# Outputs of three tiles of the last pair of heads in an idle projection bank, and gates ahead of the low parts of y

## What is computed

```python
# layer A: windowed attention, blocks of 128 queries, keys: window + context
s_lat = einsum('bqkgd,bjkd->bkgqj', qb, kb) * scale      # masked to |i-j| <= 128
s_ctx = einsum('bqkgd,bckd->bkgqc', qb, kc) * scale
p = softmax(concatenate([s_lat, s_ctx, s_sink]))
o = p_lat @ vb + p_ctx @ vc
y = (o * silu(g)) @ w_out
# layer B: neighbourhood attention, 8 rows x 16 columns of keys, with a relative bias
s = einsum('bnqhd,brnjhd->bhnqrj', q_r, k_reg) * scale + bias
p = softmax(concatenate([s, s_ctx]))
y = ((p_lat @ v_reg + p_ctx @ vc) * silu(g)) @ w_out
```

## Time and profile before

| | |
|---|---|
| median of 3 runs | 2119.71 us (2117.7 to 2121.08) |
| profiled execution | 2125.02 us, its span 2123.2 us |
| granted TensorE clock, mean | 0.979 |
| PE busy | 95% of the span |
| DVE, ACT, POOL busy | 52%, 38%, 38% |

### The profile page before, as it was taken

How to read it: one execution, slowest core, us unless ns; L and a number is a source line. 1 busy time by engine, 2 the same in 40 slices (tenths; PEclk the granted TensorE clock), 3 DMA queues, 4 the chain that set the end, 5 groups by cost and what they waited for, 6 DMA issues and landing times.

```text
span 2123.2 us, 36592 instructions
## 1 busy us (share of the span) xinstructions
PE 2011.9 (95%) x14756; PEld 1668.3 (79%) x14756; DVE 1096.0 (52%) x2212; ACT 814.4 (38%) x1584; POOL 811.5 (38%) x586
## 2 busy tenths in 40 slices
PE   7999999999998899999999899799999999999895
PEld 6878878877877788888888788678888888887674
DVE  5457467658556565556666624533344344344625
ACT  4100100100125365556666502534544545545501
POOL 3333333333346523212222145544444344354456
PEclk9999999999999999999999899899999999999997
DMA  4322332322222300101001233121111111112142
GB/s 163 136 82 90 109 98 72 119 90 70 79 90 97 103 34 21 33 34 34 34 34 57 85 108 115 65 75 50 45 46 50 48 43 50 50 41 78 53 145 113
DMA packets 48325, 155.99 MB, mean 73 GB/s; under 512 B 5280, under 2 KB 8224, under 8 KB 48032
## 3 DMA queue, kind: packets, MB, share of 16 engines
q1 hardware_dynamic: 47152, 152.40, 21.7%
q10 hardware_dynamic: 1008, 1.27, 0.2%
HBM read 132.94 MB, written 20.71 MB: 72 GB/s over the span
## 4 chain that ended last, share of the span: by engine, by line
PE 85%; DVE 7%; issue 3%; POOL 3%; ACT 2%; DMA 1%; POOLq 0%; DVEq 0%; SPq 0%; ACTq 0%
PE psum L821 23%; PE psum L822 21%; PE psum L823 21%; PE psum L996 8%; PE psum L957 7%; PE psum L973 5%; DVE win L1317 1%; PE psum L830 1%; POOL out_tile L798 1%; PE psum L923 1%; POOL w_lo L660 1%; POOL rstd L683 1%; DVE logits L1529 0%; DVE u_lo L1563 0%; DVE x_hat L1431 0%
## 5 line engine op out<-in xcount | busy, mean ns | idle before, releaser
L821 PE MATMUL psum<-u_hi,w_hi 128*128 128x512 f32 (+1 forms) x1440 | 547.5, 380 | 13.3 <-DVE u_lo L1440 7.5
L658 POOL CAST w_hi<-w_raw 128x1024 fp32r<-128x1024 f32 x140 | 155.8, 1113 | 982.2 <-DMA w_raw<-weights_in 982.2
L822 PE MATMUL psum<-u_lo,w_hi 128*128 128x512 f32 (+1 forms) x1440 | 528.2, 367 | 0.0
L823 PE MATMUL psum<-u_hi,w_lo 128*128 128x512 f32 (+1 forms) x1440 | 527.6, 366 | 0.0
L660 POOL TENSOR_TENSOR w_lo<-w_raw,w_hi 128x1024 fp32r<-128x1024 f32 x140 | 348.9, 2492 | 11.2
L821 PEld LDWEIGHTS psum<-u_hi,w_hi 128*128 128x128 f32 x1440 | 274.8, 191 | 66.8 <-issue 8.9
L823 PEld LDWEIGHTS psum<-u_hi,w_lo 128*128 128x128 f32 x1440 | 274.7, 191 | 45.4
L822 PEld LDWEIGHTS psum<-u_lo,w_hi 128*128 128x128 f32 x1440 | 275.3, 191 | 39.2
L1192 ACT ACTIVATE logits<-logits,neg_max 128x640 f32<-128x640 f32 (+2 forms) x288 | 226.1, 785 | 66.0 <-DVE neg_max L1529 64.9
L1210 ACT ACTIVATE prob_t<-psum 128x320 f32<-128x320 f32 (+1 forms) x288 | 119.0, 413 | 330.2 <-PE psum L973 330.1
L1201 ACT ACTIVATE logits<-logits,row_rec 128x640 f32<-128x640 f32 (+1 forms) x288 | 217.7, 770 | 0.0
(11 more groups left out here) (142 smaller groups left out, 3006.0 us busy)
## 6 DMA issues: line engine op xcount, KB each, us to landing
w_raw<-weights_in SPq DMA_DIRECT2D x140, 512.0 KB, 3.6
w_ada<-w_ada_in SPq DMA_DIRECT2D x48, 512.0 KB, 3.5
residual<-act_buf SPq DMA_DIRECT2D x4, 2048.0 KB, 7.4
tab<-bias_tab_in SPq DMA_DIRECT2D x16, 496.5 KB
res<-residual SPq DMA_DIRECT2D x26, 256.0 KB, 3.5
act_buf<-x_t_in SPq DMA_DIRECT2D x8, 512.0 KB, 13.5
out<-out_tile SPq DMA_DIRECT2D x8, 512.0 KB, 2.6
staged<-a_y SPq DMA_DIRECT2D x6, 640.0 KB, 2.9
```

The costliest lines, as they stand in the source:

```text
L658: pool.tensor_copy(w_hi[:, slot, :], w_raw[:, slot, :]).then_inc(w_hi_done, 1)
L821: pe.matmul(out, wh, xh, start=first, stop=False)
L822: pe.matmul(out, wh, xl, start=False, stop=False)
L823: return pe.matmul(out, wl, xh, start=False, stop=last)
```

## The change

The outputs of tiles -1, 0 and 1 go to the first 128 columns of a `pj` bank, which no projection uses in those rounds, and no longer wait for logits. The output of tile -1 waits instead for the last projection that used the bank to have been read; and PE waits in round 3, ahead of the first projection chunks, until the output of tile 1 has been gated. In all rounds of the last pair DVE does `gate_output` ahead of `low_y`.

```diff
+    def out_bank(layer, g):
+
+        aside = 0 <= g - (TILE0[layer] + (PAIRS - 1) * TILES[layer] - 1) < 3
+        return (pj[EARLY[layer][1].index % 2][:, 0:P], True) if aside else (ps_out, False)
...
@@ outputs
-            pe.wait_ge(logit_done, min(s + 6, STEP0[layer] + 2 * PAIRS * TILES[layer]))
+            out, aside = out_bank(layer, g)
+            if not aside:
+                pe.wait_ge(logit_done, min(s + 6, STEP0[layer] + 2 * PAIRS * TILES[layer]))
+            elif t == TILES[layer] - 1:
+                after(pe, pj_free[EARLY[layer][1].index % 2], EARLY[layer][1].index // 2)
...
-                    mm = pe.matmul(ps_out[r, :], v[:, tile, r], prob_t[:, g % 2, h, c, :], start=c == 0,
+                    mm = pe.matmul(out[r, :], v[:, tile, r], prob_t[:, g % 2, h, c, :], start=c == 0,
...
@@ attention (TensorE)
                 if pair == PAIRS - 1:
+                    if t == 3:
+                        pe.wait_ge(gated, g - 1)
...
@@ gate_output
-            out, y = ps_out, y_tile(layer, y_buf[layer][pair % 2], t)
+            (out, _), y = out_bank(layer, g), y_tile(layer, y_buf[layer][pair % 2], t)
...
@@ attention (VectorE)
-                if pair == PAIRS - 1:
-                    for k in {1: (0,), 2: (1, 2), 3: (3, 4), 4: (5, 6)}.get(t, ()):
-                        low_y(layer, k)
                 if layer == 0:
                     rope_due(pair, t)
                 for c in ended(PARTS[layer][pair][t]):
                     take(layer, c)
                 if g > first:
                     gate_output(layer, g - 1)
+                if pair == PAIRS - 1:
+                    for k in {1: (0,), 2: (1, 2), 3: (3, 4), 4: (5, 6)}.get(t, ()):
+                        low_y(layer, k)
```

## The result

The changed kernel took 2129.92 us (median of 6 runs, 2125.95 to 2131.83), the kernel before 2118.72 us (6 runs, 2117.7 to 2121.19). The ratio is 1.0048, 95% interval 1.0036 to 1.006. Timed again on another occasion it was 1.0044 (1.003 to 1.0057). So it is 10 to 11 us slower (11.2 by these medians, 10.2 by the ratio). The prediction said slower by 4.7 us, less than half of that, and its range ended at 2129.0 us, 0.9 us under the measured median.

The account below looks back on a forecast made before the run. A ring of engines in which only PE's waits cost time was taken as the bound. -2.5 + 3.4 us in B, -2.2 + 2.5 in A and +3.5 for the clock gave +4.7 on 2119.7: 2124.4 us, range 2118.5 to 2129.0.

Parts of the forecast that it names:

- the loss of these two rounds without the clock: Rounds 3 and 4: low parts behind the gate delay the next transposes, 3.4 us in B and 2.5 us in A.
- The whole sum at an unchanged clock: Both layers' gains until round 3 and losses behind it: +1.2 us, bounds -0.8 to +3.5.
- the clock term: Three new PE gaps of 2 us and more, each bringing 1.2 GHz in two of three cases: +3.5 us.
- The gain until round 3: Rounds 0 to 2: outputs in PE's gaps and earlier gates bring round 3's transposes forward, 2.5 us in B, 2.2 in A.
- The first: Rival: new stalls are there but the clock stays up or shorter early idle pays for it; 2120.9 us; chance 0.20.
- The second: Rival: outputs in the old gaps keep the upper clock through rounds 0 to 3 and behind new gaps; 2116.4 us; chance 0.12.
- The third: Rival: all three gaps bring the lower clock, and low parts meet a second such stretch per layer; +8.7 us, 2128.4; chance 0.10.
- The fourth: Rival: outputs wait anyway for something else, so nothing is seen there; +3 or so; chance 0.58 together with the forecast.

Follow-up runs that it names:

- the clock held up: Changed kernel plus 6 matmuls by a tile of zeros in TensorE's new gaps of rounds 4 and 5: 2124.18 us, ratio 1.0026 to the kernel before.
- the gap filled: Changed kernel, low parts before gate in rounds 3 and 4, unread matmuls before round 3's transposes: 0.9977, again 0.9985; with outputs in their old place 0.9996.
- the bank alone: Changed kernel with low parts ahead of the gate as before, outputs of tiles -1, 0 and 1 still in the projection bank: 2117.74 us, ratio 0.9992.

## Why the prediction was right or wrong

**The waits were forecast rightly, place by place.** TensorE no longer stood idle ahead of the outputs in rounds 0 to 2, the gate behind TensorE's work kept the low parts waiting in rounds 3 and 4, and the copy behind them held up the next transposes. The prediction put the loss of these two rounds without the clock at 3.4 + 2.5 = 5.9 us. Stretch II with the clock held up is 60.9, against 55.6 as the mean of the two traces of before: 5.3 us. The whole sum at an unchanged clock, +1.2 us, has no run of its own. The nearest, with the clock held up behind these gaps but not in round 3, was 5.5 us slower than before.

**The step that failed is the clock term, "3 gaps x 2/3 x 1.75 = 3.5 us".** Stretch II of the changed kernel is 66.3 us in the mean of two traces, with the clock held up 60.9: 5.4 us. Seven of eight gaps brought the lower level, and there were four gaps, not three: the fall behind round 5 of A, which the earlier trace rows show in the kernel before, was not there in its second trace, so that it was no property of before that one could leave out of the sum. The price of one, 1.5 us between two rows above, was near the 1.75 taken. The term also had nothing for round 3, whose work took 1.8 us longer in the mean of two traces (12.6 against 10.8).

**The gain until round 3 was a little too large.** The prediction gave it as 4.7 us at the transposes of round 3, 2.5 in B and 2.2 in A. There it is 3.7 us (44.8 before, 41.1 changed, each the mean of two traces). At the outputs of round 3, behind the round's work, 1.9 us of it are left (stretch I, 55.6 and 53.7).

**What took the rest is in part open.** In ten traces nothing fills the gap of round 3, and 19 of their 20 pieces of work of round 3 lie below 1.00 (0.54 to 0.82), in the kernel before as in the others, behind one long gap (4.45 us), a short one (1.84 us) or gaps in other places. In nine of these traces this work takes 11.7 to 13.5 us in both layers together; with the gap filled it is 8.6 us in each of three. So the lower level costs about 3 us there, and filling wins them back, but that the change made this worse by lengthening the gap is not shown: the changed kernel's two traces took 11.7 and 13.5 us, those of before 12.0 and 9.7, and the last, the only one with 1.00 in B, makes most of the 1.8 us. That low parts done sooner meet GpSimd's casts (5.01 us instead of the 2.87 of the first trace) put the transposes of A off by about 1 us, but the run without that gained nothing in time.

Put together: -3.7 + 1.8 + 5.3 + 5.4 = +8.8 us, and timed were 10.4 and 11.2. The four traced executions themselves are only 7.7 us apart in the mean (2121.4 and 2129.1 us), since the first of before was a long one. So the stretches hold all of the difference of these executions, and what is missing against the medians is which executions were traced.

**The rivals.** The first (the clock stays up) fell in every trace of the changed kernel. The second asked for 1.00 through rounds 1 to 5; the changed kernel's own windows show 0.65 and 0.73 in round 3 and less than 1.00 in three of four behind it. Its estimate of round 3's work at the upper level, 3.9 and 4.9 us, was right: with the gap filled it took 3.82 and 4.77. Its 0.50 for both rounds 0 and 1 of A was read too far, since the window of the earlier trace rows ends with round 0; the stretch behind it, 1169.5 to 1174.2, has 0.59 with TensorE busy for 4.63 of 4.70 us. The third was nearest in size (+8.7), by the same mechanism as the forecast with all gaps falling. The fourth (nothing to be had from the wait for logits) falls with the traces: the outputs begin behind the transposes without the 1.9 us of idle, and TensorE reaches the transposes of round 3 sooner with the bank alone. In the times the bank's worth could not be told from nothing (0.9992, with 1.0001 as the upper end). The page of the Trainium skill "TensorE: Matmul & The Clock Gate", section "HAM oscillation — how this bites in real kernels", warns of longer gaps only. Here gaps of 1.78 to 2.33 us were followed by clocks of 0.60 to 0.70 in seven of eight cases, and the measurement decides. The gap of 4.46 us ahead of round 3, which the prediction did not foresee, is of the kind that the section warns of, and 0.65 was granted behind it.

## What to carry to other kernels

On an engine with a fixed order, put work that needs nobody ahead of an instruction that waits for a slow producer, and behind one whose producer is long done; here the same swap costs 9 to 11 us through the rounds with projection work, while in the rounds without it TensorE reaches round 3 sooner by 1 to 2 us in the traces (40.5 to 41.9 against 42.9), which no time shows. So it must be decided round by round. Price an idle gap of TensorE by its length and by the clock of what follows it: a gain that only makes TensorE arrive sooner at a wait leaves a longer pause there, and here the work behind it was slow until the pause was filled. Take two traces of a kernel before sizing a gain of a few us, since here two traces of the same kernel differed by 4.3 us in the 110 us that mattered.

## What the runs showed of the hardware

TensorE matmuls whose result nobody reads, 14 in A and 9 in B placed in a gap, made the kernel faster by 2 to 4 us against the same kernel without them (ratios 0.9977 and 0.9985 against 0.9994, each to the kernel before on its own chip; the intervals of the last two overlap), with the granted clock of the work behind them at 1.00 instead of 0.70 and 0.68. Matmuls with a tile of zeros as one operand held the clock up as well (1.00 in all four windows of each of two kernels), and 14 float32 matmuls of 128 columns appear as 28 in the trace and take 3.39 us. A gap of 1.69 to 1.76 us in the scores of round 5 of A was followed by work at 1.00 in four traces and at 0.61 to 0.70 in four, so that one trace does not tell whether such a gap costs anything.

VectorE's subtraction of 128x1280 took 1.44 us (2.88 for two) alone and 2.5 us (5.01 for two) beside GpSimd's casts of the same size.
